# A decoder step on one core: one slot instead of two between two groups of attention tiles

## What is computed

```python
qb, kk, vv = arrange(q), with_prev(arrange(k)), with_prev(arrange(v))   # by stride, blocks of 128
s = einsum(qb, kk) * HEAD_DIM ** -0.5 - slopes * (dist * dilation)
s = where(valid, s, -inf)
m = max(s); p = exp(s - m); l = sum(p)
o = einsum(p / l, vv); lse = m + log(l)
```

## Time and profile before

| | us |
|---|---|
| median of 3 runs | 1792.45 (1792.27 to 1793.32) |
| the profiled execution | 1793.64 |
| its span, first to last instruction | 1791.8 |
| PE busy in the span | 1754.7 (98%) |
| ACT busy in the span | 496.5 (28%) |
| attention slots, by PE's steps | about 624 to 852 |

### The profile page before, as it was taken

One profiled execution on the slowest core, in us unless ns is written; L12 is line 12 of the kernel. 1 busy time (PEld: TensorE's weight loads), 2 busy tenths in 40 slices (PEclk: granted clock), 3 DMA queues, 4 the chain that ended last, 5 costly groups with the idle time before them and its releaser, 6 DMA issues.

```text
span 1791.8 us, 29801 instructions
## 1 busy us (share of the span) xinstructions
PE 1754.7 (98%) x12362; PEld 1715.1 (96%) x12362; DVE 830.3 (46%) x909; ACT 496.5 (28%) x901; POOL 916.2 (51%) x492
## 2 busy tenths in 40 slices
PE   7899999999999999999999998999999999999998
PEld 6899999999999999999989998999999999999997
DVE  3632314344434345445846587554445444632313
ACT  5433200101010044646102125333333332201003
POOL 3297432333333323232537438888878887344550
PEclk9899999999999999999999999999999999999999
DMA  6333311212122423454734342222322222723122
GB/s 217 109 122 127 105 50 48 74 45 75 42 78 77 165 80 128 139 177 133 220 124 126 119 137 74 72 70 82 100 76 80 84 70 63 284 87 122 54 62 95
DMA packets 166947, 187.89 MB, mean 105 GB/s; under 512 B 7225, under 2 KB 143665, under 8 KB 166873
## 3 DMA queue, kind: packets, MB, share of 16 engines
q1 hardware_dynamic: 139008, 144.27, 25.0%
q10 hardware_dynamic: 27865, 42.56, 6.9%
HBM read 133.05 MB, written 53.76 MB: 104 GB/s over the span
## 4 chain that ended last, share of the span: by engine, by line
PE 91%; DVE 4%; DMA 2%; ACT 1%; issue 1%; POOL 1%; SPq 0%; DVEq 0%; ACTq 0%; POOLq 0%
PE unit_ps L991 47%; PE pair_ps L1052 29%; PE unit_ps L1423 4%; PE task_banks L1257 2%; PE task_banks L1230 1%; PE task_banks L1243 1%; PE task_banks L1163 1%; DMA x_spill<-wide 1%; PE task_banks L1147 1%; PE task_banks L1140 1%; PE task_banks L1149 1%; DVE a_lo L2073 1%; PE task_banks L1029 0%; PE task_banks L1135 0%; PE task_banks L1120 0%
## 5 line engine op out<-in xcount | busy, mean ns | idle before, releaser
L991 PE MATMUL unit_ps<-a_hi,w_part 128*128 128x344 f32 x2976 | 602.4, 327 | 3.7 <-DVE a_lo L2073 3.4
L859 POOL TENSOR_TENSOR w_part<-w_raw,consts 128x1024 fp32r<-128x1024 f32 (+1 forms) x77 | 184.1, 2391 | 656.0 <-PE unit_ps L991 633.5
L991 PEld LDWEIGHTS unit_ps<-a_hi,w_part 128*128 128x128 f32 x2976 | 486.1, 189 | 13.0 <-issue 9.8
L991 PE MATMUL unit_ps<-a_lo,w_part 128*128 128x344 f32 x1488 | 316.4, 321 | 0.0
L991 PEld LDWEIGHTS unit_ps<-a_lo,w_part 128*128 128x128 f32 x1488 | 252.0, 189 | 0.0
L1052 PE MATMUL pair_ps<-a_hi,slots_a 128*128 128x258 f32 x1344 | 226.6, 283 | 3.4 <-DVE a_lo L2087 1.6
L862 POOL TENSOR_TENSOR w_part<-w_raw,w_part 128x1024 fp32r<-128x1024 f32 (+1 forms) x79 | 207.8, 2630 | 15.6 <-DVE a_lo L2073 9.7
L1052 PEld LDWEIGHTS pair_ps<-a_hi,slots_a 128*128 128x128 f32 x1344 | 189.3, 189 | 4.5 <-DVE a_lo L2087 1.8
L991 PE MATMUL unit_ps<-b_hi,w_part 128*128 128x344 f32 x720 | 133.4, 320 | 0.0
L1052 PE MATMUL pair_ps<-a_lo,slots_b 128*128 128x258 f32 x672 | 122.3, 284 | 1.3 <-issue 1.3
L1528 ACT ACTIVATE snap<-pair_ps 128x516 f32<-128x516 f32 x112 | 67.3, 601 | 185.1 <-PE pair_ps L1052 185.1
(11 more groups left out here) (283 smaller groups left out, 2895.4 us busy)
## 6 DMA issues: line engine op xcount, KB each, us to landing
w_raw<-in_w_in SPq DMA_DIRECT2D x46, 512.0 KB, 3.8
h_spill<-h_out SPq DMA_DIRECT2D x11, 1032.0 KB, 4.9
raw_a<-in_w_gate_up SPq DMA_DIRECT2D x11, 1024.0 KB, 7.0
raw_b<-in_w_gate_up SPq DMA_DIRECT2D x11, 1024.0 KB, 5.1
gate_spill<-stage ACTq DMA_DIRECT2D x16, 516.0 KB, 2.9
a_lo<-h_spill SPq DMA_DIRECT2D x15, 516.0 KB, 5.4
w_raw<-in_w_down SPq DMA_DIRECT2D x16, 448.0 KB, 3.6
att_in<-att_spill ACTq DMA_DIRECT2D x3, 2048.0 KB, 9.4
```

The costliest lines, as they stand in the source:

```text
L859: pool.tensor_tensor(part[:, 0], raw, one, ALU.mult).then_inc(w_high, 1)
L991: mm = pe.matmul(unit_ps[s][:, n, 0:PIECE], w_part[:, slot, w, k0 + by * k, :], x[:, k, n * PIECE:(n + 1) * PIECE], start=(k == 0 and part ...
```

## The change

The spacing of the groups becomes one slot instead of two. Before, the tiles stood in slots 0 to 7, 10 to 15 and 18 to 21; now they stand in 0 to 7, 9 to 14 and 16 to 19. The keys' turn stands in slots -1, 8 and 15 (before: -2, 8 and 16). The values' turn shares the slot of the group's first tile, 0, 9 and 16 (before: -1, 9 and 17): its first task at phase 0, the scores at phase 1, its second task at phase 2. The 14 units and their steps stay; the last two attention slots now hold no task. On ACT `values_out` and the load of the next group's values move to the head of the first tile's slot, ahead of its exponentials, and the last tile's `rows_out` is no longer put off.

```diff
-SLOT_OF = {n: n + 2 * g for g in range(GROUPS) for n in GROUP_TILES[g]}
+SLOT_OF = {n: n + g for g in range(GROUPS) for n in GROUP_TILES[g]}
-K_SLOT = {SLOT_OF[GROUP_TILES[g][0]] - 2: g for g in range(GROUPS)}
-V_SLOT = {SLOT_OF[GROUP_TILES[g][0]] - 1: g for g in range(GROUPS)}
-SLOTS = range(-2, SLOT_OF[TILES - 1] + 2)
+K_SLOT = {SLOT_OF[GROUP_TILES[g][0]] - 1: g for g in range(GROUPS)}
+V_SLOT = {SLOT_OF[GROUP_TILES[g][0]]: g for g in range(GROUPS)}
+SLOTS = range(-2, 23)
...
-        _first = [("v", V_SLOT[_s], _i) for _i in range(V_PAIRS)]
+        _first = [("v", V_SLOT[_s], 0)] + _first + [("v", V_SLOT[_s], 1)]
...
+                    if phase == 0 and s in V_SLOT:
+                        turn_values(V_SLOT[s], 0)
                     if phase == 1 and s in TILE_IN:
                         tile_scores(TILE_IN[s])
+                    if phase == 2 and s in V_SLOT:
+                        turn_values(V_SLOT[s], 1)
...
-                    if s in V_SLOT and 1 <= phase <= V_PAIRS:
-                        turn_values(V_SLOT[s], phase - 1)
...
             def att_steps(s):
 
+                if s in V_SLOT:
+                    g = V_SLOT[s]
+                    values_out(g)
+                    if g < GROUPS - 1:
+                        load_values(g + 1)
                 n = TILE_IN.get(s)
                 if n is not None:
                     exponentials(n)
...
-                if s - 1 in TILE_IN and s < SLOTS[-1]:
+                if s - 1 in TILE_IN:
                     rows_out(TILE_IN[s - 1])
-                if s in V_SLOT:
-                    g = V_SLOT[s]
-                    values_out(g)
-                    if g < GROUPS - 1:
-                        load_values(g + 1)
...
-            rows_out(TILES - 1)
```

## The result

The changed kernel took **1808.0 us** (median of six runs, 1807.0 to 1809.0), the kernel before 1793.0 beside it (1792.3 to 1794.4). The ratio is 1.0083, interval 1.0070 to 1.0095: 15.0 us slower. Forecast were 1809, range 1801.5 to 1814.5, slower with 0.92. The profiled executions, 1793.64 and 1808.66, differ by 15.0 too.

The account below looks back on a forecast made before the run. PE, busy for 98% of the span, was taken to bound the kernel. Waits of 6.9, 2.9 and 2.1 (11.9 us) plus 4.6 for the clock gave 16.5 on the median 1792.45: 1809 us, range 1801.5 to 1814.5.

Parts of the forecast that it names:

- The bound: Whole kernel: PE busy 98% of the span, full over slots 8 and 9, so next to nothing to win.
- Scores: Scores of each group's first tile: PE waits for ACT's values' copies, 3.3 at tile 8, 1.1 at tile 0, none in group 2.
- The second values task: Groups 1 and 2: the task's second half waits 0.3 us for DVE's bias work.
- Turns: Turns wait for ACT's exponentials: tile 0 1.8 us, tile 8 3.5, group 2's first about 1.5, its next 0.4.
- stood with tile 16: Group 2: Sigmoid block said to follow tile 14's exponentials, delaying the next ones; PE waits 0.4, between 0 and 1.5.
- The term for the issues: ACT, between values' copies and exponentials: DMA issues take 0.97 in group 0, 1.50 in group 1, 0.73 in group 2.
- Table loads: ACT's table switches: 1.28 us each without the skill's drain; with it the sum would be 4.1 us higher.
- The clock: Group 1: waits at tile 8's scores and turn each drop PE's clock to half; 4.6 us, between 0 and 10.
- the second drop: Clock drop at the turn of tile 8: 2.6 us; the one ahead of its scores 2.0, partly covered by the turn's wait.
- rival B: The clock drops at groups 0 or 2 too: 1814 us; chance 0.13.
- A: The waits come but the clock holds: 1804.4 us on the median; chance 0.25.
- C: Slots 0 and 9: ACT's values' copies done in time, so not slower, 1791 to 1795 us; chance 0.08.

Follow-up runs that it names:

- copies_first: The changed kernel with ACT's Silu of slot -1 and Sigmoid block of slot 8 moved behind the copies of the first values task: 1801.4 us.
- issues_late: The changed kernel with the values' rows store and the next group's values load issued behind the exponentials of a group's first tile: 1803.9 us.
- table_early: The changed kernel with the edits of copies_first and issues_late, plus one tiny Exp behind the moved Silu and Sigmoid blocks: 1795.4 us.
- fill: The changed kernel with 20 unused matmuls on PE ahead of the scores of tile 8 and 14 ahead of its turn: 1805.6 us.
- g1_again_b: Third profiled execution of the kernel with new spacing at group 1's border only, groups 0 and 2 as in the kernel before: 1801.97 us.
- ladder: The kernel before with added ACT copies ahead of the exponentials of tiles 1, 3, 6 and 12, so four turns inside groups wait: 1803.4 us.

## Why the prediction was right, point by point

**The bound.** Right. PE had 0.23 us idle in the attention; there was nothing to win, and behind the last tile nothing was given back: 200 us of the late stages (845 to 1045 before, 860 to 1060 after) hold 198.95 busy in both kernels.

**Scores.** Tile 8: forecast 3.3, measured 3.33. Tile 0: 1.1 against 1.22. Tile 14: none, and none seen. That the Sigmoid block and the Silu are the cause is shown by `copies_first`. Reading the order on ACT was enough.

**The second values task.** Forecast 0.3 in groups 1 and 2. No list shows them, since they lie inside a row of merged matmuls, but the durations do: in group 2 the second task lasts 1.45 where the first lasts 1.06, some 0.4, and in group 1 of `copies_first`, at full clock, 1.49 where the first lasts 1.12. In group 1 of the changed kernel PE was at half clock and the 1.77 of the task can't be split.

**Turns.** Tile 0: 1.8 forecast, 1.12 + 0.36 measured; tile 8: 3.5 against 2.39 + 0.91; tile 14: 1.5 against 0.34 + 0.91; tile 15: 0.4 against 0.53, released by the copy of tile 14's outputs right behind the exponentials. The Sigmoid block on that path is the block of slot 16, as the earlier trace rows shows; the prediction's words "stood with tile 16" name the wrong place, and its sum doesn't need them. The term for the issues is shown by `issues_late`; that the table load counts is shown by `table_early`, which took 0.6 off the turn of tile 0 and 0.6 off that of tile 8. All of it together: 11.9 forecast, 11.0 measured, with the 0.4 inside the values task of group 2 beside it.

**Table loads.** The Trainium skill (ScalarE: Activation LUTs, What ACT_TABLE_LOAD costs) adds a drain to each switch of tables. In the changed kernel the load at 724.78 again stands 0.02 behind the end of the windows, and the first Exp 1.29 behind the start of its load at 738.38. The estimate with that drain, 4.1 higher, would have been 1813.

**The clock.** The mechanism held and the sum is near, 4.6 against some 4.0 (4.9 with all of the busy time); its parts were mis-sized. I gave the second drop 2.6 and the first 2.0, since the wait at the turn was to cover a part of the first. It covers nothing: the exponentials stand a fixed time behind the second values task, and that task itself came late at half clock. In `fill` the turn of tile 8 begins 2.4 us earlier in the window (135.9 us behind its start against 138.3), and the stretch in which PE waits or fills ahead of it is about as long (2.55 against 2.39); so the first drop cost some 2.4. By its length it could have cost more: 6.8 us with PE busy in 6.3 of them, about 3.1 lost; at full clock the second values task holds a wait of some 0.4 (1.49 against 1.12 in `copies_first`), which may be hidden at half clock. The second drop, with some 3.3 busy, lost about 1.6. The first came out above its 2.0 and the second below its 2.6, so that the sum is near is in part luck. `fill` shows that the clock has this price beside the waits, g1_again_b that it varies. The 3.38 and 1.55 of the earlier trace rows were good guides to which single waits count: the ladder has 1.65 on the one side and 2.07 on the other. The 0.93 and 0.91 of `issues_late`, shorter than 1.55 and followed by a drop, do not fit them. My rival B needed drops at groups 0 or 2; there were none behind 1.22, 1.12 + 0.36 or 0.34 + 0.91.

**Rivals.** A (1804.4) falls with the two stretches at 0.50 and with `fill`. C had its condition made true by `copies_first`: then the scores wait no more, but the turns do, because C had left out the issues and the table load ahead of the exponentials; its upper end, 1795, is nearly reached only when these are moved too (1795.4).

## What to carry to other kernels

Where a task is moved closer to the work that feeds it, walk the in-order stream of the engine that must empty its banks, and add what stands there between the feeding task and the copy: blocks of another function, table loads and DMA issues count each with its row. A slot without a small task, which costs the bounding engine nothing, may be the slack that another engine needs. Price a new wait of PE twice, as the wait and as the matmuls that may run at half clock behind it, and take the second as a range.

## What was not expected of the hardware

A single wait of 2.07 us, with PE full before and behind, was followed by 0.50 of the clock for some 3.5 us, and 1.65 was not, in two executions each. Two waits of 0.93 and 0.91 were followed by a drop where one of 3.33 had ended nine us earlier, and waits of 0.92 and 0.91 were not where it hadn't, in one execution each. The same 3.33 was followed by 7 us at 0.50 in two executions and 3.5 in a third of the same kernel. DMA issues of 0.70 and 0.64 on ACT's queue held up the table load by 1.49 when they stood ahead of it, and nothing when they stood behind the exponentials.
